# Twenty-two small parameter loads moved to the queue of the weight loads, and the first modulation units reordered on TensorE

## What is computed

```python
def ada_modulate(x, c, norm_g, ada_w, ada_b):
    ada = jax.nn.silu(c) @ ada_w + ada_b
    shift, scale, gate = jnp.split(ada, 3, axis=-1)
    h = rmsnorm(x, norm_g) * (1.0 + scale[:, None, :]) + shift[:, None, :]
    return h, gate[:, None, :]

def even_layer(x, c, norm_g, ada_w, ada_b, in_w, ...):
    h, gate_res = ada_modulate(x, c, norm_g, ada_w, ada_b)
    a, u, v, gate = _split(h @ in_w, EVEN_SIZES)
    ...
```

## Time and profile before

| | us |
|---|---|
| median of three runs | 945.32 |
| lowest and highest of them | 945.25, 945.72 |
| the profiled execution | 946.93 |
| its span | 943.9 |
| PE busy | 915.9 (97%) |
| DVE busy | 638.7 (68%) |
| ACT busy | 517.4 (55%) |

### The profile page before, as it was taken

One profiled execution on the slowest core, in us unless ns is written; L12 is line 12 of the kernel. 1 busy time (PEld: TensorE's weight loads), 2 busy tenths in 40 slices (PEclk: granted clock), 3 DMA queues, 4 the chain that ended last, 5 costly groups with the idle time before them and its releaser, 6 DMA issues.

```text
span 943.9 us, 19566 instructions
## 1 busy us (share of the span) xinstructions
PE 915.9 (97%) x8685; PEld 889.3 (94%) x8685; DVE 638.7 (68%) x736; ACT 517.4 (55%) x610; POOL 2.1 (0%) x14
## 2 busy tenths in 40 slices
PE   7899999999999999999999999999889999999998
PEld 7899999999999999899899999899879999999997
DVE  2897887775577456567689886556777665465565
ACT  3446444545654567863475654367656653454445
POOL 0000000000000000000000000000000000000000
PEclk9999999999999999999999999999999999999999
DMA  9999547874667543367444453334535567556521
GB/s 338 365 366 343 178 159 232 282 247 136 199 207 239 157 149 111 122 193 244 150 135 149 140 163 91 91 91 135 159 101 177 157 200 224 178 179 203 175 92 45
DMA packets 153439, 172.30 MB, mean 183 GB/s; under 512 B 4000, under 2 KB 137692, under 8 KB 153228
## 3 DMA queue, kind: packets, MB, share of 16 engines
q1 hardware_dynamic: 151696, 167.43, 54.9%
q10 hardware_dynamic: 1660, 3.63, 1.1%
HBM read 170.00 MB, written 1.05 MB: 181 GB/s over the span
## 4 chain that ended last, share of the span: by engine, by line
PE 50%; DVE 5%; ACT 2%; issue 1%; DVEq 0%; POOL 0%; POOLq 0%; ACTq 0%
PE pj L2635 40%; PE pj L2591 1%; DVE w_lo L1449 1%; PE pj L2593 1%; PE pj L2592 1%; PE m_all L2327 1%; PE m_all L2310 1%; ACT w_hi L949 1%; PE pj L2420 1%; PE m_all L2313 0%; PE m_all L2252 0%; ACT work L1369 0%; DVE work L1877 0%; DVE small L1878 0%; DVE spare L1732 0%
## 5 line engine op out<-in xcount | busy, mean ns | idle before, releaser
L1449 DVE TENSOR_TENSOR w_lo<-raw,w_hi 128x2048 fp32r<-128x2048 f32 (+1 forms) x126 | 285.3, 2268 | 139.2 <-ACT w_hi L949 138.5
L2635 PE MATMUL pj<-h_hi,w_hi 128*128 128x256 f32 (+1 forms) x1208 | 343.0, 284 | 3.8 <-DVE h_lo L1888 1.5
L2635 PE MATMUL pj<-h_lo,w_hi 128*128 128x256 f32 (+1 forms) x1208 | 337.2, 279 | 0.0
L2635 PE MATMUL pj<-h_hi,w_lo 128*128 128x256 f32 (+1 forms) x1208 | 336.9, 279 | 0.0
L949 ACT ACTIVATE w_hi<-raw 128x2048 fp32r<-128x2048 f32 (+1 forms) x126 | 237.9, 1890 | 51.9 <-PE pj L2635 27.0
L2635 PEld LDWEIGHTS pj<-h_hi,w_hi 128*128 128x128 f32 (+1 forms) x1208 | 225.9, 187 | 7.8 <-issue 5.4
L2635 PEld LDWEIGHTS pj<-h_lo,w_hi 128*128 128x128 f32 (+1 forms) x1208 | 226.0, 187 | 0.4
L2635 PEld LDWEIGHTS pj<-h_hi,w_lo 128*128 128x128 f32 (+1 forms) x1208 | 225.9, 187 | 0.2
L2635 PE MATMUL pj<-y_hi,w_hi 128*128 128x256 f32 x592 | 166.0, 280 | 2.7 <-DVE y_lo L1977 1.9
L2635 PE MATMUL pj<-y_lo,w_hi 128*128 128x256 f32 x592 | 165.2, 279 | 0.0
L2635 PE MATMUL pj<-y_hi,w_lo 128*128 128x256 f32 x592 | 165.0, 279 | 0.0
(11 more groups left out here) (410 smaller groups left out, 1091.9 us busy)
## 6 DMA issues: line engine op xcount, KB each, us to landing
raw<-in_odd_in_w_dram SPq DMA_DIRECT2D x28, 1024.0 KB, 5.3
raw<-in_w_in_dram SPq DMA_DIRECT2D x23, 1024.0 KB, 5.3
raw<-in_ada_w_dram SPq DMA_DIRECT2D x22, 1024.0 KB, 7.5
raw<-in_w_ff_in_dram SPq DMA_DIRECT2D x16, 1024.0 KB, 5.3
raw<-in_w_ff_out_dram SPq DMA_DIRECT2D x16, 1024.0 KB, 5.2
raw<-in_even_in_w_dram SPq DMA_DIRECT2D x13, 1024.0 KB, 5.2
raw<-in_even_out_w_dram SPq DMA_DIRECT2D x8, 1024.0 KB, 5.9
raw<-in_odd_out_w_dram SPq DMA_DIRECT2D x8, 1024.0 KB, 5.5
```

What stands on the lines that cost most here:

```text
L1449: V.tensor_tensor(lo[:, 0:n], raw_of(u)[:, 0:n], hi[:, 0:n].bitcast(F32), ALU.subtract).then_inc(done, 1)
L2635: m = nc.tensor.matmul(to, a_, b_, start=(s == 0 and q == 0 and (fb == 0 or not together)), stop=(s == len(steps_) - 1 and q == 2), skip_g ...
```

## The change

- SP issues the 22 row loads, after u5 and ahead of u6; ACT issues none.
- x is copied from PSUM by ACT (parts 0 and 2) and DVE (parts 1 and 3). ACT squares x when all four parts are there.
- On PE 8 instead of 5 matmuls without a use stand ahead of the transposes of x and none behind. n0 no longer waits for x; n4 does (it writes a PSUM bank in which x stood).
- In the schedule `modulate` 0 stands right behind n4, and `ev_first` behind it: PE multiplies k-steps 0 to 3 of ev 0. Its k-steps 4 to 7 stay where the job stood. n5's sum on DVE thereby stands behind `modulate` 0.
- On PE n6 (u7) runs ahead of n5 (u6). For DVE both come at u7's place.

```diff
@@ program: the schedule
     step("ada_half", 0)
     ada(0, 0, 1, 0)
+    step("modulate", 0)
+    step("ev_first")
     ada(0, 0, 1, 1)
-    step("modulate", 0)
     ada(0, 1, 1, 0)
     ada(0, 1, 1, 1)
@@ walking the schedule
+        sixth, seventh = (u["order"] for u in units if u["ada"] is not None and u["ada"][2] in (5, 6))
+        ada_turn = {sixth: (), seventh: (seventh, sixth)}
...
                 elif kind == "ada" and ada_part:
-                    ada_part(what)
+                    for u in ada_turn.get(what, (what,)):
+                        ada_part(u)
@@ SP
             def load_all_rows():
-                act.wait_ge(S("rows_zero"), 1)
+                sp.wait_ge(S("rows_zero"), 1)
...
-                    act.dma_start(rows[r:r + src.shape[0], half, 0:src.shape[1]], src).then_inc(S("rows_loaded"), 16)
+                    sp.dma_start(rows[r:r + src.shape[0], half, 0:src.shape[1]], src).then_inc(S("rows_loaded"), 16)
...
             for u, un in enumerate(units):
+                if u == 6:
+                    load_all_rows()
@@ ACT
-                for q in range(4):
+                for q in (0, 2):
                     act.wait_ge(S("x_turned"), q + 1)
...
-                squares(0, x, E_["sq"], lambda e, q: e.wait_ge(S("x_ready"), q + 1), load_all_rows)
+                act.wait_ge(S("x_ready"), 4)
+                for q in range(4):
+                    nc.scalar.activation(ar(E_["sq"] + 2 * q, 2), x[:, 2 * q:2 * q + 2, :], ACT.Square).then_inc(S("squares"), 1)
+                plain_root(0)
@@ DVE
+            def load_x():
+                for q in (1, 3):
+                    dve.wait_ge(S("x_turned"), q + 1)
+                    V.tensor_copy(x[:, 2 * q:2 * q + 2, :], M[q][:, :].rearrange("p (c t) -> p c t", c=2)).then_inc(S("x_ready"), 1)
@@ PE
-                for _ in range(5):
+                for _ in range(8):
                     nc.tensor.matmul(M[1][:, 0:T], K("ones"), cst[:, 0:T], start=True, stop=True)
...
-                for _ in range(4):
-                    nc.tensor.matmul(PJ[1][:, 0:T], K("ones"), cst[:, 0:T], start=True, stop=True)
...
-                if n == 0:
+                if n == 4:
                     pe.wait_ge(S("x_ready"), 4)
...
+            def ev_first():
+                run_job(("ev", 0), range(KD // 2))
...
+                if key == ("ev", 0) and rows_in is None:
+                    rows_in = range(KD // 2, KD)
...
+                    if rows_in is not None and s not in rows_in:
+                        continue
```

## The result

The changed kernel takes 950.47 us (median of 4 runs, 949.01 to 950.99) against 945.39 for the kernel before (median of 4; the 945.32 above is that of three of them): a ratio of 1.0041, interval 1.0029 to 1.0054. Seven further runs of it gave 950.22. It is **slower by 4 to 5 us**, where 946.5, no measurable change, was forecast. The profiled execution took 949.01 us with a span of 947.3, against 946.93 and 943.9: the spans differ by 3.4, the times by only 2.1, because 3.0 us lay outside the span before and 1.7 lie there now. The spans are what can be followed, and the other runs of the changed kernel have longer ones still, 947.9 to 948.9.

What follows compares the result with a forecast made beforehand. Bounds: PE's order of work and the saturated weight stream in the opening. n7 ends at 38.3 (PE 38.1, data 38.3) against 37.16: +1.15 us; 946.93 + 1.15 = 948.1, less 1.61 for a median: 946.5 us, range 944.4 to 949.0.

Steps and rivals of the forecast that it cites:

- The rest: PE's wait covers that: 0.: Opening on PE: n0 to n3 each move under 1 us, covered by PE's wait for the rows (2.92 us, then 1.5).
- The row loads on SP: SP's queue: first load ends at 16.6, others 0.36 us each, u6 issued at 24.1, last row landing at 25.5.
- The torn stream: Weight stream behind the row loads: u6 meets nearly idle DMA engines, lands at 29.3; u8 at 34.4, 1.7 us later.
- The first rival: Stream not torn: first row load not blocked, n7 ends at 36.8, 0.4 us sooner, time 944.9; chance 0.22.
- u10 and u12 ... the stream has work queued: 0.: Later weight units: both issued ahead of u9's and u11's landing, so the reordered sums cost the stream 0.
- rows plus 12.6: PE from turning the rows to the end of n7: 12.6 us, so rows at 25.5 give 38.1.
- The term for half of ev 0: PE ahead of n7: 24 matmuls put in, adding 3.0 us.
- near tie: End of n7: PE's own work gives 38.1, u8's data 38.3; the later counts, 1.15 us later than 37.16.
- The end moves by as much as the end of n7.: Chain through DVE from n7's end to PE's restart at 43.20 stays 6.04 us, so n7's shift carries to the end.
- From the profiled execution to the median: Last step of the sum: the median lies 1.61 us below the profiled execution, so 948.1 becomes 946.5.
- slower issues: Rival, SP's row loads: 0.41 us each gives 947.5, with a 1.40 us stall too 948.6; chance 0.27.
- the ceiling of 1.4 us: PE's start on u13, set by the DMA stream: slack limits any gain to 1.4 us.

Runs made afterwards that it cites:

- e1: Changed kernel plus eight useless matmuls on PE ahead of its wait for the rows, to hold the clock: 947.65 us, ratio 1.0023.
- e11: Kernel before with only the x part of the change (copied by two engines, n0 not held for it), rows by ACT, old order: 945.39 us, ratio 0.9996.
- e3: Kernel before with one part of the change alone, SP issuing the 22 row loads ahead of u6: 947.73 us, ratio 1.0019.
- e5: Changed kernel with SP issuing the row loads ahead of u3 instead of u6: 947.79 us, ratio 1.0018.
- e7: Kernel before with the row loads alone changed, issued by SP ahead of u3: 947.71 us, ratio 1.0022.
- e4: Changed kernel with the old order: no early half of ev 0, n5 ahead of modulate 0 and n6: 947.63 us, ratio 1.0026.
- e8: Changed kernel with the old order and eight useless matmuls ahead of PE's wait for the rows: 948.37 us, ratio 1.0024.
- e2: Changed kernel with the 22 row loads issued by ACT again, behind its squares of x: 947.55 us, ratio 1.0019.
- e10: Changed kernel with ACT issuing the row loads right behind the load of x: 946.02 us, ratio 0.9999.
- e9: Kernel before with ACT issuing the row loads right behind the load of x: 946.48 us, ratio 0.9999.

## Why the prediction was wrong, step by step

**"The rest: PE's wait covers that: 0."** This step failed. The parts that let n0 to n3 start sooner did so: n3 ends at 22.45, and the wait that was to shrink to 1.5 us grew from 2.92 to 4.17. I called that wait a cover and never asked what PE does in it. Just behind it PE was on the 1.2 GHz level (0.81 from 26 to 28 us, 0.50 from 28 to 30), and n4 took 5.36 us. e1 shows that it is the clock: rows and stream nearly the same, n4 3.74, n7 1.4 us sooner, the median 2.6 to 2.8 lower. In the windows of the kernel before the granted clock was 1.00 throughout the opening, and I took that for a constant. That the wait grew is not the whole reason: in e11 it shrank to 2.07 us and the clock fell too.

**The row loads on SP.** The first was forecast to be held for 2.7 to 3 us and was held for 1.44; the 0.36 us for the others were 0.34. The issue of u6 came at 22.36, 1.7 us before the forecast. The rows should then have been turned at 23.7, and came at 26.63: the last was issued at 22.02, and PE's wait for it ended 4.6 us later, not 1.7. A landing time taken from a load in an idle queue (128 KB in 2.2 us) was used for loads queued behind megabytes. The gain of 1.4 us on the rows was 0.3. This is the second term that failed.

**The torn stream.** Right in kind, near in size. The mean share from 22 to 26 us is 0.85, and these are the landing times of u6, issued at 22.36, and of u8, issued some 1 us later at 23.36 (us from issue to landing):

```profile
raw<-in_ada_w_dram SPq DMA_DIRECT2D x1, 1024.0 KB, 6.2
...
raw<-in_ada_w_dram SPq DMA_DIRECT2D x1, 1024.0 KB, 10.6
```

u6 lands at 28.6 and u8 at 34.0; forecast 29.3 and 34.4, before 27.3 and 32.7. The first rival, a stream that isn't torn, is refuted for SP's queue, by this, e3, e5 and e7. The reason that the prediction gave, an idle queue, is at most a part of it, since in e7 the engines are busy at 114 GB/s.

**"u10 and u12 ... the stream has work queued: 0."** u10 was issued (34.83) ahead of u9's landing (36.8), as the prediction says, and the stream thinned out all the same, to 237 and 266 GB/s. The term was wrong, and was not paid for only because PE was later still.

The Trainium skill (DMA: Bandwidth & Descriptors, "Issuing engines are not separate DMA queues") holds that DMAs of different issuers interleave on the same engines and that spreading them saves little but issue time. It calls that time usually small beside the DMA. By that rule the move of the rows to SP would have been worth nothing to the stream but the issue time. The traces agree with it for the loads by ACT (376 GB/s from 20 to 22 us in the kernel before, while the last of them were issued). For the same loads ahead of the units in one queue the issue time is not small: 22 of them hold SP from 13.69 to 22.36, and u6 is issued 5.45 us later than before. Whether the issue time is all of the loss was not separated.

**The sum for PE.** The rule "rows plus 12.6" gives 26.63 + 12.6 = 39.2 and with the 1.6 us of the clock 40.9; n7 ended at 40.47. The term for half of ev 0 was therefore right (32.02 to 34.95, 2.9 us for 3.0). Of the 2.4 us between 38.1 and 40.47 the late rows are 1.1 and the clock up to 1.6. What I had as a near tie between PE (38.1) and u8's data (38.3) was decided by PE, with 3 us of its own work more on the path.

**"The end moves by as much as the end of n7."** Right, and it made the rest readable: 3.3, 3.3 and 3.4 us in the profiled execution.

**From the profiled execution to the median.** I took off 1.61 us, the difference for the kernel before. For the changed kernel 1.46 are to be added (950.47 - 949.01): its executions differ, and the one more that was profiled had the clock low for longer. The sum for a median had no term for an effect that is not the same in every execution. What lies outside the span differs too (3.0 us in the profiled execution before, 1.8 in the median of the later runs), and most of the 1.61 comes from that.

**The range.** It reached to 949.0 by way of slower issues, a mechanism that did not occur. The cases were all about when data arrive; none was about how fast PE is when they do.

What the measurements add up to, by the end of n7: 37.16 before; 38.1 to 38.4 with the torn stream in the old order, whatever the clock does (e3, e4, e8); 39.07 with the new order on top and the clock held (e1); 40.47 and 41.48 with the low clock as well (the changed kernel). That is some 1.1 us for the stream, 0.7 for the order and 1.4 to 2.4 for the clock, which costs nothing in the old order. The medians say the same more coarsely: 2.0 to 2.6 us lost in e3, e4, e8 and e1, 4 to 5 with all three; they don't resolve the 0.7 of the order. With the stream whole at u6 to u8 and the rows late, the new order with its low clock loses some 2 us (e2 against e11). With the rows early in ACT's queue (e10) all of it is gone.

**Open** are three points. Which property of the row loads slows the units behind them in the same queue wasn't separated (their number, their size, their packets' targets). Of the 2 us that e3 and e7 lose in the median, n7's end explains 0.9. And why the clock falls in one kernel or execution and not in another at like waits isn't known. No kernel here was measurably faster than the one before. Of the ceiling of 1.4 us, e10 reached 0.8 in its profiled execution, and there the ceiling itself had come down to that.

## What to carry to other kernels

- A wait is only a cover if the engine comes out of it as it went in: work that is moved forward ahead of a fixed wait makes the wait longer, and on PE that may cost more than it hides. Look at the granted clock behind each wait of a few microseconds, and put a term for it into the sum if the wait grows.
- Keep small loads out of the queue that feeds a saturated stream; in a second queue, and early, the same loads cost nothing here.
- When the order of use changes, ask which place each load waits for: a sum that is made later frees its place later, and the next unit is issued later.
- When work is put ahead of a step on which the rest hangs, work out both sides of that step, data and engine, with the worst value of each: it decides whether another loss is hidden or paid.

## What the runs showed of the hardware

- **Small loads ahead of large ones in one queue.** 22 loads of up to 24 KB in SP's queue cut the stream to 116 GB/s for 2 us and 290 for 2 more (e3: 110 and 325), and u8 came 1.3 us late. With them in ACT's queue the rate from 20 to 26 us stayed at 376 GB/s or more (before, e2). In e7 the engines were busy (1.17) at 114 GB/s, in the changed kernel 0.78 at 116.
- **Issue times.** A small load costs SP 0.34 us from issue to issue, as it does ACT (0.36), and the issue itself takes 0.29 us for 4 KB and 0.37 for a 1 MB unit: the size hardly counts. The issue of u5, right behind that of u4, took 5.20 us, and the first row load behind it 1.44.
- **The clock after a wait.** PE waited 2.92 us in the kernel before and kept 1.00. It waited 4.17 us in the changed kernel, 3.86 in e3, 2.07 in e11 and 2.02 in e2, and n4 behind it took 5.2 to 5.4 us instead of 3.74; at 3.37 us (the changed kernel once more) it took 6.10. The length of this wait alone does not tell. Eight matmuls of 256 columns, for which PE was busy 3.62 us ahead of the wait (0.52 us then left of it), kept the clock at 1.00 (e1).
- **The clock near the end.** In every profile it falls once more, not before 936 us, when PE has little left to do. The last 16 transposes took 1.95 us in the kernel before and 3.56 in e9.
- **Scatter.** The mean granted clock differs between executions of one kernel: 0.993 to 1.000 in 88 executions of the kernel before, with times from 944.9 to 949.4 us. The three with 0.993 or 0.994 were 1.0 to 3.5 us above the median, but the 32 with 1.000 still spread over 2 us. So the clock is a part of the scatter that limits what can be measured here, and not all of it.
